# A conformer layer with product-key experts: both expert halves from fetched rows for the last 128 tokens, and a dense first half for 416

## The chip, the cores and the metric

The kernel runs on one core of one Trainium2 chip. The metric is the device time of one execution in microseconds (us). A core has TensorE (PE in the profile, PEld its weight loads), VectorE (DVE), ScalarE (ACT), GpSimd (POOL) and SyncE (SP), and 16 DMA engines that all queues share.

## The reference

One layer of an encoder for 544 tokens (a prompt of 512 and 32 of a running stream), model width 2048, all in fp32. The part around the change is the second half of the layer, a layer of single-neuron experts:

```python
def peer(h, w_pq, sub_k1, sub_k2, u_tab, v_tab):        # h = rms_norm(x, norm2_g)
        q = (xb @ w_pq).reshape(PEER_BLOCK, PEER_HEADS, PEER_DKEY).astype(f32)   # 8 heads, 128 wide
        s1 = jnp.einsum('thd,nd->thn', q[..., :half], sub_k1.astype(f32))        # 128 keys each
        s2 = jnp.einsum('thd,nd->thn', q[..., half:], sub_k2.astype(f32))
...
        sc, j = lax.top_k(cand, PEER_TOPK)                                       # 16 of 256 candidates
        idx = jnp.take_along_axis(cidx, j, axis=-1)                              # expert = i1 * 128 + i2
        g = jax.nn.softmax(sc, axis=-1)
        ue = u_tab[idx]
        ve = v_tab[idx]
        a = jnp.einsum('td,thkd->thk', xb, ue).astype(f32)
        wgt = (g * jax.nn.gelu(a, approximate=False)).astype(xb.dtype)
        return jnp.einsum('thk,thkd->td', wgt, ve)
```

There are 16384 experts, so u_tab and v_tab (peer_u, peer_v) are 16384 x 2048; a token uses 8 x 16 = 128 of them. Ahead of it stand a projection of 9216 columns with convolution and attention, two output projections that are merged with gates, `w_out`, and the residual.

## The kernel before

**Numbers.** Every large product is made of three fp32r products. ACT rounds a loaded block of weights (`w_raw`, 128x2048) to `w_hi` (L546), POOL makes the rest `w_lo = w_raw - w_hi` (L482), and PE adds hi·hi, lo·hi and hi·lo. A *unit* is one such block: 16 slices of 128 rows against 544 tokens, held as two halves of 272, so 96 matmuls (L1280). Weights and their parts have two buffers. Loops are hardware loops, two units a round, and engines meet only by semaphores that count; each engine runs its program in its written order.

**Stages.** Stage 1 (39 to 1093 us) has 72 units, in four head pairs of 18: projection, convolution on DVE (L877), attention. `evac` on DVE (L784 to L808) takes a unit's result out of PSUM, and the next unit but one needs that space. Then come merge (16 units, 1093 to 1317 us), out (16, to 1509), PQ (the query projection, 8, to 1603), U (128 units of peer_u, to 3216) and V (16 groups of 8 blocks of peer_v, to 4450).

**U stage.** Each unit gives 128 experts' activations for all 544 tokens: ACT copies them out of PSUM (L708), POOL scales them by the RMS factor `rs2` (L500), ACT applies Gelu (L712) and stores them to `a_scr`. The first 40 units have the top-k of five tiles of tokens on DVE between them (L1066 to L1120), eight units to a tile; PE waits for a tile's choice in a hook in the next tile's seventh unit (L1507 to L1509). After them follow 26 blocks of 16 tokens, three units each, in which one-hot matmuls (L1532) turn the chosen gates into a dense gate matrix `g_scr`; DVE makes the one-hot operands (L1147 to L1149) and takes the results (L1162, L1164). Ten units more end the stage.

**V stage.** For the first 416 tokens activations times gates are multiplied densely with peer_v, 384 matmuls of 416 columns a group (L1557). For the last 128 tokens POOL fetches for each of the 128 slots one row of peer_v per token (`rows`, L506, from `v_rows`) and the single activation (`elements`, L513, from `a_scr`), and DVE weighs them (L1202) and adds row times weight (`gather_add`, L1208). In this stage DVE makes `w_lo` (L1196).

**Rows of peer_v.** The table in `w_all` is stored in blocks for PE; `v_rows` is a copy of it as rows, made in stage 1 by SP: two DRAM-to-DRAM transfers of 1 MB for each unit (`rows_of`, L334), behind the unit's load of `w_raw` (L316), on SP's one queue.

Of the kernel before, what the change touches and what calls it, by code (L numbers as in the profile page):

```python
# [20 lines left out]
F32 = mybir.dt.float32  # L21
F32R = mybir.dt.float32r
# [4 lines left out]
P = 128  # L27
# [36 lines left out]
NVG = 3  # L64
# [36 lines left out]
def build(nc, w_all, x_t, consts, late, params, lams, keys_t, past_k, past_v, hist,  # L101
          y_t, k_t, v_n, cst_p, cst_s):
    ctx = ExitStack()
    with ctx:
# [44 lines left out]
        oraw = ay.take("oraw", [P, T])  # L149
        az = Area(MT, MEND - MT)  # L150
# [7 lines left out]
        rs1 = az.take("rs1", [P, T])  # L158

# [23 lines left out]
        h2_lo = ao.take("h2_lo", [P, KD, T], F32R)  # L183
        aq = Area(MT, MEND - MT)
# [8 lines left out]
        ab = au.take("ab", [P, 2, T])  # L193
        gb = au.take("gb", [P, 2, T])
        v_idx = au.take("v_idx", [P, SLOTS], U32)
        a_idx = au.take("a_idx", [P, SLOTS], U32)
        gate_g = au.take("gate_g", [P, SLOTS])
        a_el = au.take("a_el", [P, SLOTS])
        w_g = au.take("w_g", [P, SLOTS])
        gsum_g = au.take("gsum_g", [P, NH])  # L200
        p_col = au.take("p_col", [P, 1])
# [3 lines left out]
        g_hi = ag.take("g_hi", [P, T], F32R)  # L205
# [20 lines left out]
        oh2 = aw.take("oh2", [P, 8, NKEY], F32R)  # L226
        oh1 = aw.take("oh1", [P, 8, 2, NKEY], F32R)

        avx, avy = Area(X0, BIG), Area(Y0, BIG)
        acc = avx.take("acc", [P, KD, T])  # L230
        a_st = avy.take("a_st", [P, GRP, NT])
# [21 lines left out]
        g_scr = nc.dram_tensor("g_scr", (NGB, P, NKEY, GB), F32, kind="Internal").ap()  # L253
        v_rows = nc.dram_tensor("v_rows", (NGRP, GRP, P, DM), F32, kind="Internal").ap()
# [37 lines left out]
        ab_full, ab_scaled, gelu_done = sem("ab_full"), sem("ab_scaled"), sem("gelu_done")  # L292
# [12 lines left out]
        vg_loaded, vg_taken = [sem(f"vg_loaded{i}") for i in range(NVG)], sem("vg_taken")  # L305
        el_loaded = [sem("el_loaded0"), sem("el_loaded1")]
# [6 lines left out]
        def _(sp):  # L313
# [17 lines left out]
            def rows_of(hp, g, n):  # L331
# [43 lines left out]
            with sp.Fori(0, NH // 2) as hp:  # L375
                z_loads(hp)
# [1285 lines left out]
```

## Time and profile before

| what | value |
|---|---|
| median of 3 runs | 4459.39 us (4457.0 to 4462.22) |
| profiled execution, its time and its span | 4454.38 us, 4452.6 us |
| busy share of the span | PE 98%, DVE 67%, POOL 39%, ACT 24% |
| moved by DMA | 822.58 MB |
| mean granted clock of TensorE | 0.989 of full speed |

The span is from the first to the last instruction of the profiled execution. Busy times of PE are modelled and overlap (two matmuls in the pipe), so the pace of PE is read from the starts of its instructions. A `xN` behind an instruction says that N of them are drawn together. What ended an engine's idle time stands behind an arrow.

### The profile page before, as it was taken

The numbers are of one execution on the slowest core, as the hardware profiler recorded it, in microseconds if no ns is written. First come the engines' busy times: TensorE is split into PE (matmuls) and PEld (weight loads), VectorE is DVE, ScalarE is ACT, GpSimd is POOL, SyncE is SP. The second block draws the span as 40 slices with busy tenths as digits, with TensorE's granted clock in tenths as the row PEclk, the third lists the DMA queues.
The fourth block names the chain that finished last, engine by engine and source line by source line (L and its number), as shares of the span: only waits on it lengthen the run. The fifth ranks groups of instructions, "written<-read, shape, count | busy, mean of one in ns | idle before, by whom it ended". The sixth has DMA issues, their size and how long they took to land.

```text
span 4452.6 us, 78681 instructions
## 1 busy us (share of the span) xinstructions
PE 4351.6 (98%) x30758; PEld 4276.9 (96%) x30758; DVE 3003.3 (67%) x4653; ACT 1079.1 (24%) x1100; POOL 1758.2 (39%) x639
## 2 busy tenths in 40 slices
PE   8999999999999999999999999999989999999999
PEld 7999999999999999999999999999989999999999
DVE  5767656676762256557888888886268777877774
ACT  3332323322211122222222222222212121221221
POOL 3323323332333344444444444444544433444420
PEclk9999999999999999999999999999999999999999
DMA  6656566564333322222333333333577767776763
GB/s 241 235 191 229 197 234 229 188 227 164 106 136 135 110 95 108 108 106 102 133 126 136 131 130 135 134 135 128 198 277 264 291 261 292 266 296 258 282 253 126
DMA packets 332184, 822.58 MB, mean 185 GB/s; under 512 B 23152, under 2 KB 230768, under 8 KB 264688
## 3 DMA queue, kind: packets, MB, share of 16 engines
q1 hardware_dynamic: 279968, 608.53, 39.0%
q0 software_dynamic: 22528, 134.30, 7.4%
q10 hardware_dynamic: 29520, 77.40, 4.5%
q8 instruction: 119, 1.95, 0.2%
q14 instruction: 49, 0.40, 0.0%
HBM read 734.72 MB, written 219.66 MB: 214 GB/s over the span
## 4 chain that ended last, share of the span: by engine, by line
issue 56%; PE 21%; POOL 18%; DMA 3%; DVE 1%; POOLq 0%; ACT 0%; DVEq 0%; SPq 0%; ACTq 0%
PE pair L1557 21%; POOL w_lo L482 13%; POOL ab L500 4%; DMA a_el<-a_scr,a_idx 3%; POOL vg L506 1%; DVE ST L1208 1%; DVE acc L1192 0%; POOL a_el L513 0%; DMA xs<-x_t 0%; POOL xsq L488 0%; POOLq L481 0%; ACT h_hi L552 0%; POOLq L497 0%; POOLq L492 0%; DVE w_lo L1196 0%
## 5 line engine op out<-in xcount | busy, mean ns | idle before, releaser
L482 POOL TENSOR_TENSOR w_lo<-w_raw,w_hi 128x2048 fp32r<-128x2048 f32 x242 | 1118.0, 4620 | 1114.6 <-ACT w_hi L546 1114.6
L1280 PE MATMUL pair<-h_hi,w_hi 128*128 128x272 f32 x6656 | 1397.5, 291 | 12.8 <-issue 12.8
L1280 PE MATMUL pair<-h_hi,w_lo 128*128 128x272 f32 x6656 | 1381.5, 289 | 0.0
L1280 PE MATMUL pair<-h_lo,w_hi 128*128 128x272 f32 x6656 | 1377.0, 288 | 0.0
L1280 PEld LDWEIGHTS pair<-h_hi,w_hi 128*128 128x128 f32 x6656 | 1048.2, 189 | 21.1 <-issue 13.9
L1280 PEld LDWEIGHTS pair<-h_lo,w_hi 128*128 128x128 f32 x6656 | 1048.5, 189 | 0.0
L546 ACT ACTIVATE w_hi<-w_raw 128x2048 fp32r<-128x2048 f32 x368 | 703.8, 1913 | 1417.3 <-PE pair L1557 858.4
L1280 PEld LDWEIGHTS pair<-h_hi,w_lo 128*128 128x128 f32 x6656 | 1044.7, 189 | 0.0
L1557 PE MATMUL pair<-wt_hi,w_hi 128*128 128x416 f32 x2048 | 727.3, 355 | 49.4 <-DVE acc L1192 48.3
L1557 PE MATMUL pair<-wt_hi,w_lo 128*128 128x416 f32 x2048 | 728.7, 356 | 0.0
L1557 PE MATMUL pair<-wt_lo,w_hi 128*128 128x416 f32 x2048 | 722.6, 353 | 0.0
L506 POOL DMA_INDIRECT vg<-v_rows,v_idx x128 | 321.1, 2508 | 595.7 <-DVE ST L1208 584.9
L500 POOL TENSOR_TENSOR ab<-ab,rs 128x544 f32<-128x544 f32 x128 | 178.7, 1396 | 791.0 <-ACT ab L708 791.0
L1557 PEld LDWEIGHTS pair<-wt_hi,w_hi 128*128 128x128 f32 x2048 | 389.7, 190 | 57.3 <-DVE acc L1192 53.2
L1557 PEld LDWEIGHTS pair<-wt_lo,w_hi 128*128 128x128 f32 x2048 | 390.3, 191 | 6.3
L1557 PEld LDWEIGHTS pair<-wt_hi,w_lo 128*128 128x128 f32 x2048 | 389.5, 190 | 3.2
L708 ACT ACTIVATE ab<-pair 128x544 f32<-128x544 f32 x128 | 80.1, 626 | 1203.5 <-PE pair L1280 1203.5
L1148 DVE TENSOR_SCALAR oh<-late_sb,i_t,g_hi 128x128 fp32r<-128x128 f32 x416 | 356.5, 857 | 0.0
L877 DVE SCALAR_TENSOR_TENSOR xg<-u,params_sb,xg 128x512 f32<-128x512 f32 x464 | 338.6, 771 | 23.3 <-DVE xg L875 1.3
L1192 DVE TENSOR_TENSOR acc<-pair,acc 128x416 f32<-128x416 f32 x256 | 149.4, 588 | 277.0 <-PE pair L1557 218.0
L1208 DVE SCALAR_TENSOR_TENSOR ST<-vg,w_g,ST 128x2048 f32<-128x2048 f32 x128 | 300.6, 2348 | 2.9 <-DVE w_g L1202 2.9
L1196 DVE TENSOR_TENSOR w_lo<-w_raw,w_hi 128x2048 fp32r<-128x2048 f32 x126 | 287.9, 2285 | 13.3 <-ACT w_hi L546 13.3
(223 smaller groups left out, 3999.6 us busy)
## 6 DMA issues: line engine op xcount, KB each, us to landing
w_raw<-w_all SPq DMA_DIRECT2D x368, 1024.0 KB
v_rows<-w_all SPq DMA_DIRECT2D x128, 1024.0 KB, 8.8
a_scr<-gb ACTq DMA_DIRECT2D x128, 272.0 KB, 2.1
g_scr<-g_st ACTq DMA_DIRECT2D x26, 1024.0 KB, 4.1
a_st<-a_scr SPq DMA_DIRECT2D x16, 1664.0 KB, 8.4
gl_st<-g_scr SPq DMA_DIRECT2D x16, 1664.0 KB
gate_scr<-zb ACTq DMA_DIRECT2D x32, 272.0 KB, 2.2
gt<-gate_scr SPq DMA_DIRECT2D x32, 272.0 KB, 3.4
```

The costliest lines, as they stand in the source:

```text
L482: pool.tensor_tensor(w_lo[:, slot, :], raw[:, slot, :], w_hi[:, slot, :].bitcast(F32), ALU.subtract)\
L500: pool.tensor_tensor(ab[:, n, :], ab[:, n, :], rs2[:, :], ALU.mult).then_inc(ab_scaled, 1)
L506: pool.indirect_dma_start(vg[j % NVG][:, :], None, v_rows.rearrange("g c p d -> (g c p) d"), bass.IndirectOffsetOnAxis(v_idx[:, j:j + 1], ...
L546: act.activation(w_hi[:, slot, :], raw[:, slot, :], ACT.Copy).then_inc(hi_ready, 1)
L708: act.activation(two(ab[:, n, :]), PV[n], ACT.Copy).then_inc(ab_full, 1)
L877: own.by(V.scalar_tensor_tensor(xg[:, a:b], src, cw, xg[:, a:b], ALU.mult, ALU.add))
L1148: V.tensor_scalar(oh1[:, sl, 0, :], iota, c1, g_hi[:, bass.ds(t, 1)].bitcast(F32), ALU.is_equal, ALU.mult)
L1192: V.tensor_tensor(acc[:, d, 0:NT], PD[k], acc[:, d, 0:NT], ALU.add).then_inc(acc_added, 1)
L1196: V.tensor_tensor(w_lo[:, slot, :], raw[:, slot, :], w_hi[:, slot, :].bitcast(F32), ALU.subtract)\
L1208: V.scalar_tensor_tensor(acc_g, vg[x % NVG][:, :], w_g[:, bass.ds(s0 + x, 1)], acc_g, ALU.mult, ALU.add)\
L1280: last = mm(out[:, f, :], a, b[:, k, f * HT:(f + 1) * HT], start=(x == 0 and y == 0), stop=(x == n - 1 and y == 2))
L1557: last = mm(PD[k], a, r_[b][:, c, :], start=(c == 0 and y == 0), stop=(c == GRP - 1 and y == 2))
```

## The change

Five things are changed together.

1. **U for 416 tokens.** Units of peer_u are multiplied with the first 416 tokens only, 48 matmuls of 416 columns (`u_unit`). `h2` is scaled by `rs2` before PQ (DVE `h2_s`, ACT rounds, DVE subtracts, slice by slice), so ACT applies Gelu directly from PSUM (`u_slot`) and L500 and L708 fall away.
2. **Rows of peer_u.** In stage 1 SP also loads the 128 blocks of peer_u (`u_load`, 1 MB each, two a unit in 16 of a head pair's 18 units), DVE transposes each in 32x32 pieces (`turn`, at the head of `evac`), and SP stores it to `u_rows` by four transfers of 32 partitions (`u_store`). The copies to `v_rows` move to the loops of merge, out, PQ and U. The merge's inputs `c_all` and `o_lo` make room: they are stored to `c_scr` and `o_scr` in stage 1 and loaded again at its end.
3. **Dots.** For the last 128 tokens POOL fetches rows of peer_u (`fetch`, nine in a round of two gate blocks, three buffers `rows`) and DVE makes one dot product per slot with `h2_g` in PSUM (`dot`, 128x2048). 128 matmuls ahead of the gate blocks (`h2_turned`, at the end of unit 41) put `h2` there with tokens on partitions.
4. **Gate blocks.** They begin at unit 42 instead of 40. One-hot matmuls are fp32 with 128 columns, where they were fp32r with 256; L1148 falls away; the results are copied out by ACT (`gate_copy`) and no longer by DVE. DVE makes `w_lo` of every second unit there (L1248), POOL of the others.
5. **V stage.** Fetched activations and their weighing are gone: one Gelu over the dots on ACT and one product with the gates on DVE stand ahead of the stage.

```diff
--- before.py
+++ after.py
...
         SV, TOV = S[:, :, 0:HT], TO[:, :, 0:HT]
 
         def two(ap):
@@ -251,6 +260,9 @@
         x2_scr = nc.dram_tensor("x2_scr", (KD, P, T), F32, kind="Internal").ap()
         a_scr = nc.dram_tensor("a_scr", (NKEY, P, T), F32, kind="Internal").ap()
         g_scr = nc.dram_tensor("g_scr", (NGB, P, NKEY, GB), F32, kind="Internal").ap()
+        c_scr = nc.dram_tensor("c_scr", (KC, P, T), F32, kind="Internal").ap()
+        o_scr = nc.dram_tensor("o_scr", (KC, P, T), F32, kind="Internal").ap()
+        u_rows = nc.dram_tensor("u_rows", (NKEY, 4, 32, 4, DM // 4), F32, kind="Internal").ap()
...
+            def u_load(hp, i):
+                sp.dma_start(u_in[:, i % 2, :], w_all[bass.ds(hp * 32 + (i + U_PU), 1)].rearrange("a p n -> p (a n)"))\
+                    .then_inc(u_loaded[i % 2], 16)
+
+            def u_store(hp, i):
+                for q in range(4):
+                    sp.dma_start(u_rows[bass.ds(hp * 32 + i, 1), :, :, q, :].rearrange("a b i n -> i (a b) n"),
+                                 u_out[32 * q:32 * q + 32, i % 2, :].rearrange("p (b n) -> p b n", b=4)).then_inc(u_stored[i % 2], 16)
...
+                        for k in range(2):
+                            if n <= 16:
+                                sp.wait_ge(u_turned, hp * 32 + (2 * n + k + 1))
+                            if n < 16:
+                                u_load(hp, 2 * n + k)
+                            if 1 <= n <= 16:
+                                u_store(hp, 2 * n + k - 2)
...
+            for s in u_stored:
+                sp.wait_ge(s, 64 * NKEY // 2 + 1)
+            sp.wait_ge(o_stored, 16 * (NH - 1) + 1)
+            sp.wait_ge(c_stored, 32 * (NH - 1) + 1)
+            sp.dma_start(o_lo[:, 0:NH - 1, :].bitcast(F32), o_scr[0:NH - 1].rearrange("c p n -> p c n")).then_inc(o_loaded[0], 16)
+            sp.wait_ge(c_stored, 32 * NH + 1)
+            sp.dma_start(c_all[:, :, :], c_scr.rearrange("c p n -> p c n")).then_inc(c_loaded, 16)
+            sp.wait_ge(o_stored, 16 * NH + 1)
...
+            def turn(hp, i):
+
+                dve.wait_ge(u_loaded[i % 2], hp * 256 + 16 * (i // 2 + 1))
+                dve.wait_ge(u_stored[i % 2], hp * 1024 + (64 * (i // 2) + 1))
+                V.transpose(u_out[:, i % 2, :].rearrange("p (b k j) -> p k b j", b=4, k=KD), u_in[:, i % 2, :])\
+                    .then_inc(u_turned, 1)
...
             def evac(hp, r, i):
+
+                for k in range(2):
+                    if ZPH * r + i < 16:
+                        turn(hp, 2 * (ZPH * r + i) + k)
 
...
+            for k in range(KD + 1):
+                if k < KD:
+                    V.tensor_tensor(h2_s[:, k, :], h2_s[:, k, :], rs2[:, :], ALU.mult).then_inc(h2_scaled, 1)
+                if k > 0:
+                    dve.wait_ge(h2_rounded, k)
+                    V.tensor_tensor(h2_lo[:, k - 1, :], h2_s[:, k - 1, :], h2_hi[:, k - 1, :].bitcast(F32), ALU.subtract)\
+                        .then_inc(h2_ready, 1)
             with dve.Fori(0, NQ // 2) as v:
...
-            def elements(j):
-                b = j // PER_GRP
-                if b >= 2 and j % PER_GRP == 0:
-                    pool.wait_ge(el_loaded[b % 2], 16 * PER_GRP * (b // 2))
-                pool.indirect_dma_start(a_el[:, j:j + 1], None, a_scr.rearrange("c p (n o) -> (c p n) o", o=1),
...
+            def fetch(j):
+
+                if j >= NG:
+                    pool.wait_ge(row_taken, j - NG + 1)
+                table = u_rows.rearrange("c b i q n -> (c b i) (q n)") if j < SLOTS else v_rows.rearrange("g c p d -> (g c p) d")
+                pool.indirect_dma_start(rows[j % NG][:, :], None, table,
+                                        bass.IndirectOffsetOnAxis(v_idx[:, j % SLOTS:j % SLOTS + 1], 0))\
+                    .then_inc(row_loaded[j % NG], 16)
 
             pool.wait_ge(idx_ready, 1)
+            for s in u_stored:
+                pool.wait_ge(s, 64 * NKEY // 2 + 1)
+            pool.wait_ge(scores_taken, TT)
+            pool.wait_ge(chosen, TT)
+            j = 0
+            for v in range(NGB // 2):
+                for k in range(3):
+                    w = U_PU + U_G0 + 6 * v + 2 * k + 2
+                    for i in range(DOTS // 3):
+                        fetch(j)
...
-            def u_slot(v, n):
+            def u_slot(v, n, src):
                 m = v * 2 + n
                 act.wait_ge(unit_done, m + (1 + NZ + NO + NQ))
-                act.activation(two(ab[:, n, :]), PV[n], ACT.Copy).then_inc(ab_full, 1)
+                act.wait_ge(a_stored[n], v * 16 + 1)
+                act.activation(gb[:, n, :], src[n], ACT.Gelu).then_inc(ab_full, 1)
                 hi(v + (U_PU // 2 + 1), n)
-                act.wait_ge(ab_scaled, m + 1)
-                act.wait_ge(a_stored[n], v * 16 + 1)
-                act.activation(gb[:, n, :], ab[:, n, :], ACT.Gelu).then_inc(gelu_done, 1)
-                act.wait_ge(gelu_done, m + 1)
-                act.dma_start(a_scr[bass.ds(m, 1)].rearrange("a p n -> p (a n)"), gb[:, n, :]).then_inc(a_stored[n], 16)
+                act.wait_ge(ab_full, m + 3)
...
+            def gate_copy(v, gq):
+
+                b, t0 = gq // 4, 4 * (gq % 4)
+                act.wait_ge(grp_done, v * 8 + (gq + 1))
+                if gq % 4 == 0:
+                    act.wait_ge(g_stored[b], v * 16 + 1)
+                act.activation(g_st[:, b, :, t0:t0 + 4], ST[:, 2 + gq % 2, :].rearrange("p (c t) -> p c t", t=4), ACT.Copy)\
...
+            def dot(v, i):
+
+                j = v * DOTS + i
+                dve.wait_ge(row_loaded[i % NG], v * (16 * DOTS // NG) + 16 * (i // NG + 1))
+                buf = rows[i % NG]
+                V.scalar_tensor_tensor(buf[:, :], buf[:, :], 1.0, h2_g, ALU.mult, ALU.mult,
+                                       accum_out=dot_g[:, bass.ds(j, 1)]).then_inc(row_taken, 1)
+
             def g_round(v, more):
...
-                    b = gq // 4
-                    dve.wait_ge(grp_done, v * 8 + (gq + 1))
-                    if gq % 4 == 0:
-                        dve.wait_ge(g_stored[b], v * 16 + 1)
-                    part = (S, TO)[gq % 2][:, :, :].rearrange("p a n -> p (a n)").rearrange("p (t h c) -> p t h c", t=4, h=2)
-                    t0 = 4 * (gq % 4)
-                    dst = g_st[:, b, :, t0:t0 + 4].rearrange("p c t -> p t c")
-                    own.by(V.tensor_copy(dst, part[:, :, 0, :]))
-                    settle()
-                    V.tensor_tensor(dst, dst, part[:, :, 1, :], ALU.add).then_inc(grp_taken, 1)
-                    if more or gq < 6:
-                        one_hot(v, gq + 2)
-
-            one_hot(0, 0)
-            one_hot(0, 1)
+                def next_hot(gq):
+                    if more or gq < 4:
+                        dve.wait_ge(grp_done, v * 8 + (gq + 1))
+                        one_hot(v, gq + 4)
+
...
+            def u_unit(v, n, dst, hooks=None):
                 pe.wait_ge(lo_ready, v * 2 + (n + 1 + U_PU))
                 pe.wait_ge(ab_full, v * 2 + (n + 1))
-                product(PV[n], n, 0, range(KD), h2_hi, h2_lo, hooks).then_inc(unit_done, 1)
+                for k in range(KD):
+                    wh, wl = (w[:, n, k * P:(k + 1) * P] for w in (w_hi, w_lo))
+                    for y, (a, b) in enumerate(((wh, h2_hi), (wh, h2_lo), (wl, h2_hi))):
+                        last = mm(dst[n], a, b[:, k, 0:NT], start=(k == 0 and y == 0), stop=(k == KD - 1 and y == 2))
+                    if hooks and k in hooks:
+                        hooks[k]()
+                last.then_inc(unit_done, 1)
+
+            def h2_turned():
+
+                for k in range(KD):
+                    for q in range(4):
+                        for y, src in enumerate((h2_hi, h2_lo)):
+                            last = mm(PA[:, q, 32 * k:32 * k + 32], src[:, k, NT:T].bitcast(F32), ident[:, 32 * q:32 * q + 32],
+                                      start=(y == 0), stop=(y == 1))
+                last.then_inc(h2g_ready, 1)
```

On SP's queue, in stage 1, these rows stand between one load of weights and the next. Before:

```order
L316 DMA w_raw<-w_all 128x2048
L334 ISA
L334 DMA v_rows<-w_all 128x8x256
L334 ISA
L334 DMA v_rows<-w_all 128x8x256
L343 REGISTER_ALU
```

After, of which the second half repeats for the unit's second block:

```order
L331 DMA w_raw<-w_all 128x2048
L372 REGISTER_ALU
L355 ISA
L355 DMA u_in<-w_all 128x2048
L360 ISA
L360 DMA u_rows<-u_out 32x4x512
L360 ISA
L360 DMA u_rows<-u_out 32x4x512
L360 ISA
L360 DMA u_rows<-u_out 32x4x512
L360 ISA
L360 DMA u_rows<-u_out 32x4x512
```

Two copies have become two loads and eight stores, and a wait for DVE's transposes (`u_turned`) has come onto this queue behind each load of weights.

On DVE, in stage 1, this is the place between the last instruction of attention's softmax and `evac`'s first multiplication. Before:

```order
L851 SCALAR_TENSOR_TENSOR e<-e,small 128x256
L788 REGISTER_ALU
L796 REGISTER_ALU
L808 TENSOR_TENSOR zb<-pair,rs_74 128x544
```

After:

```order
L949 SCALAR_TENSOR_TENSOR e<-e,small 128x256
L873 REGISTER_ALU
L874 REGISTER_ALU
L875 STREAM_TRANSPOSE u_out<-u_in 128x16x4x32 x2
L886 REGISTER_ALU
L894 REGISTER_ALU
L906 TENSOR_TENSOR zb<-PA,rs_78 128x544
```

Two transposes, each behind waits for its load and for the four stores before it, have come ahead of the multiplication that frees the unit's PSUM.

On DVE, in the gate blocks, this is one stretch of a round of two blocks after the change (`rows` are the fetched rows, `oh` the one-hot operands, `PA` holds `h2_g`):

```order
L1248 TENSOR_TENSOR w_lo<-w_raw,w_hi 128x2048
L1254 ISA
L1256 ISA
L1256 SCALAR_TENSOR_TENSOR rows_133,dot_g<-rows_133,PA 128x2048
L1263 ISA
L1241 ISA
L1241 TENSOR_SCALAR oh_130<-late_sb,i_t 128x128
L1242 ISA
L1242 TENSOR_SCALAR oh_131<-late_sb,i_t,e_t 128x128
```

Before there were only L1147 to L1149 and the copies here; a split and nine dots a round have come in between, each dot behind a wait for its fetched row, and the one-hot operands stand behind them.

## Rows read from the trace of the kernel before

**Rows 1.** Windows by stage: us, busy us (instructions) per engine, clock, DMA share, GB/s.
```profile
39.00:1093.00 1054.00, 1041.16 (x7790) 993.79 (x7789) 690.48 (x986) 317.41 (x474) 326.27 (x72) 0.99 0.61 211
...
1603.00:3216.00 1613.00, 1612.05 (x12882) 1609.79 (x12881) 1162.28 (x2526) 403.64 (x411) 768.43 (x255) 1.00 0.35 126
3216.00:4450.00 1234.00, 1183.95 (x6160) 1166.46 (x6160) 892.33 (x887) 244.62 (x129) 456.30 (x258) 0.98 0.70 261
```

**Rows 2.** Timeline of PE, U stage: start us, us, instruction, count.
```profile
2107.74 0.28 PE L1532 MATMUL ST<-oh,oh 128*128 128x256 f32 x1
2107.86 0.41 PE L1280 MATMUL pair<-h_hi,w_hi 128*128 128x272 f32 x2
2108.11 0.41 PE L1280 MATMUL pair<-h_lo,w_hi 128*128 128x272 f32 x2
```

**Rows 3.** Waits, V stage: who, for whom, us in total, times, longest.
```profile
DVE w_g L1202 <- DMA a_el<-a_scr,a_idx: 89.7, 14, 14.3
...
PE pair L1557 <- DVE acc L1192: 48.3, 14, 11.4
```

**Rows 4.** Chain that ended last, its last piece: start us, us.
```profile
4376.84 72.55 PE pair L1557 x384
```

**Rows 5.** Timeline of PE, fp32 score matmuls in the U stage.
```profile
1704.26 3.50 PE L1499 MATMUL ST<-ksb,qp 64*128 64x128 f32 x32
1707.69 0.52 PE L1280 MATMUL pair<-h_hi,w_hi 128*128 128x272 f32 x2
```

**Rows 6.** Timeline of DVE, top-k of token tile 0, first and last instruction.
```profile
1707.89 1.22 DVE L1066 COPY sc<-ST 128x1024 f32<-128x1024 f32 x1 [20.32 <-PE ST L1499]
...
1767.73 2.29 DVE L1120 TENSOR_REDUCE isel<-wk 128x128 f32<-128x2048 f32 x1
```

**Rows 7.** Timeline of PE, the matmuls that wait for that top-k.
```profile
1782.96 0.27 PE L1509 MATMUL ST<-consts_sb,ssub 128*128 128x128 f32 x1
```

**Rows 8.** Groups by line on DVE, 2020 to 3080 us (busy us, mean ns; idle before).
```profile
L1149 DVE TENSOR_SCALAR oh<-late_sb,i_t,e_t 128x128 fp32r<-128x128 f32 x412 | 183.0, 444 | 0.0
L1147 DVE TENSOR_SCALAR oh<-late_sb,i_t 128x128 fp32r<-128x128 f32 x413 | 154.9, 375 | 0.0
```

**Rows 9.** Groups by line, V stage.
```profile
L1208 DVE SCALAR_TENSOR_TENSOR ST<-vg,w_g,ST 128x2048 f32<-128x2048 f32 x128 | 300.6, 2348 | 2.9 <-DVE w_g L1202 2.9
L1196 DVE TENSOR_TENSOR w_lo<-w_raw,w_hi 128x2048 fp32r<-128x2048 f32 x126 | 287.9, 2285 | 13.3 <-ACT w_hi L546 13.3
```

**Rows 10.** Timeline of DVE, stage 1 (in brackets idle before, and releaser).
```profile
779.93 1.97 DVE L877 SCALAR_TENSOR_TENSOR xg<-u,params_sb,xg 128x512 f32<-128x512 f32 x4
...
782.45 6.23 DVE L877 SCALAR_TENSOR_TENSOR xg<-u,params_sb,xg 128x512 f32<-128x512 f32 x4
```

**Rows 11.** Timeline of POOL in the same stretch.
```profile
783.02 4.55 POOL L482 TENSOR_TENSOR w_lo<-w_raw,w_hi 128x2048 fp32r<-128x2048 f32 x1 [10.09 <-ACT w_hi L546]
```

**Rows 12.** Windows inside stage 1 and the V stage.
```profile
400.00:600.00 200.00, 195.72 (x1486) 188.72 (x1485) 133.83 (x187) 62.19 (x87) 63.69 (x14) 0.99 0.61 208
...
3400.00:3800.00 400.00, 383.46 (x1985) 377.37 (x1984) 304.32 (x299) 80.53 (x42) 166.12 (x94) 0.98 0.74 276
```

**Rows 13.** DMA issues: KB each, median us from issue to landing.
```profile
v_rows<-w_all SPq DMA_DIRECT2D x128, 1024.0 KB, 8.8
...
g_scr<-g_st ACTq DMA_DIRECT2D x26, 1024.0 KB, 4.1
...
x_scr<-x ACTq DMA_DIRECT2D x16, 272.0 KB, 2.1
```

**Rows 14.** Timeline of PE, end of a head pair in stage 1.
```profile
829.56 0.79 PE L1280 MATMUL pair<-h_hi,w_hi 128*128 128x272 f32 x2 [4.53 <-issue]
...
834.61 0.41 PE L1280 MATMUL pair<-h_hi,w_lo 128*128 128x272 f32 x2
```

**Rows 15.** Timeline of PE, from stage 1 into the merge.
```profile
1100.51 0.64 PE L1280 MATMUL pair<-o_hi,w_hi 128*128 128x272 f32 x2 [2.30 <-DVE zb L808]
```

**Rows 16.** Timeline of DVE, from out into PQ.
```profile
1507.56 4.50 DVE L1022 COPY osq<-osum 128x544 f32<-128x544 f32 x1 [0.21 <-DVE osum L1019]
```

More of the change, by code:

```diff
@@ L158, in build @@
         rs1 = az.take("rs1", [P, T])
+        c_ts = az.take("c_ts", [P, TS])
         xs = Area(Y0, HALF).take("xs", [P, KD, T])
@@ L183, in build @@
         h2_lo = ao.take("h2_lo", [P, KD, T], F32R)
+        h2_s = Area(X0 + HALF, HALF).take("h2_s", [P, KD, T])
         aq = Area(MT, MEND - MT)
@@ L535, in _ @@
+            w = U_PU + U_G0 + BU * NGB + 1
+            while w < U_PV + 2:
+                pool.wait_ge(lo_ready, w)
+                lo(w, w % 2)
+                w += 1
+                for i in range(2):
+                    if j < SLOTS:
+                        fetch(j)
+                        j += 1
+            pool.wait_ge(rows_stored, 16 * NV)
+            for j in range(SLOTS, 2 * SLOTS):
+                fetch(j)
         @block.scalar
@@ new lines, in g_round @@
+            def g_round(v, more):
+                def next_hot(gq):
+                    if more or gq < 4:
+                        dve.wait_ge(grp_done, v * 8 + (gq + 1))
+                        one_hot(v, gq + 4)
+                un = v * 6 + (U_PU + U_G0 + 1)
+                dots = iter(range(DOTS))
+                for b in range(2):
+                    for i in range(BU):
+                        if (BU * b + i) % 2 == 0:
+                            split(un + (BU * b + i), 1)
+                        dot(v, next(dots))
+                        next_hot(4 * b + i)
+                        if i < 2 - b:
+                            dot(v, next(dots))
+                    next_hot(4 * b + 3)
@@ L1170, in _ @@
+            for gq in range(4):
+                one_hot(0, gq)
+            dve.wait_ge(h2g_ready, 1)
             with dve.Fori(0, NGB // 2 - 1) as v:
-                own.loop(v, 8)
                 g_round(v, True)
-            own.endloop(NGB // 2 - 1)
             g_round(NGB // 2 - 1, False)
+            for i in range(SLOTS - NGB // 2 * DOTS):
+                dot(NGB // 2, i)
             def prep(parity, c):
@@ L1214, in _ @@
                 prep(0, c)
+            dve.wait_ge(a_g_ready, 1)
+            own.by(V.tensor_tensor(w_g[:, :], gate_g[:, :], a_el[:, :], ALU.mult))
+            settle()
             dve.wait_ge(unit_done, NZ + NO + NQ + NU)
@@ L1218, in group @@
             def group(g, parity, more, slots, splits, pre=None):
-                s0, full, rounds, n_slots = slots
+                s0, rounds, n_slots = slots
                 for n in range(GRP):
@@ L1426, in merge_unit @@
                     product(PV[k], n, KC * k, range(KC), rhs_hi, rhs_lo, hooks and hooks[k]).then_inc(tile_done, 1)
-            with pe.Fori(0, NA // 4) as v:
+            for n in range(2):
+                merge_unit(0, n, 0, o_hi, o_lo, ({KC - 2: lambda: pe.wait_ge(o_loaded[1], 16)}, {KC - 1: mean}) if n == 0 else None)
+            with pe.Fori(1, NA // 4) as v:
                 for n in range(2):
```

281 lines of the change are left out of this document (150 added, 131 removed).

## The prediction, made before the changed kernel had run

> **What bounds the kernel now.** I read the windows by stage first. PE is busy in 1041 of the 1054 us of stage 1, in 1612 of 1613 us of U and in 1184 of 1234 us of V [rows 1]. So in U nothing but PE's own work counts; in V some 50 us are waits, and in stage 1 about 13. DVE stands at 690 of 1054 us in stage 1 and the DMA engines at a share of 0.61 with 211 GB/s [rows 1]: neither bounds now, and the change loads both. The timeline of PE gives the pace of U: a pair of 272-column matmuls starts every 0.25 us (2107.86, 2108.11 [rows 2]), so 48 pairs, a unit, take 12.0 us; the window's 1613 us less 49 for one-hot matmuls and 17 for scores (priced below) give 12.09 for each of 128 units. I take 12.02. The chain's last piece shows 416 columns: 384 matmuls in 72.55 us, 188.9 ns each [rows 4]. The waits of the V stage name DVE's `w_g` for fetched activations, 89.7 us in 14 groups, and behind it PE for DVE's `acc`, 48.3 us in the same 14 [rows 3].
>
> **U.** A unit becomes 48 x 188.9 ns = 9.07 us; 128 units give 128 x (12.02 - 9.07) = **-378 us**. Removed on ACT and POOL is work beside PE, worth nothing by itself; Gelu from PSUM takes the copy's place. Added:
> - One-hot matmuls become fp32. 32 passes of 128 columns in fp32 took 1707.69 - 1704.26 = 3.43 us [rows 5], a block's 16 matmuls have 32 such passes; the fp32r ones took 0.118 us each (2107.74 to 2107.86 [rows 2]), 1.89 a block. 26 x 1.54 = **+40**.
> - `h2_turned`: 256 passes of 32 columns. Nothing in the trace is this small; by columns it is a quarter of 107 ns, 7 us in all, and by passes 27. A pass of 32 columns still loads its weights, so I take **+22**.
> - The top-k. DVE takes 1707.89 to 1770.02, 62.2 us with its end [rows 6]; PE asks for it at 1782.96 [rows 7], 6.25 units after the scores, and finds it ready. 6.25 units are now 56.7 us, so PE waits 5.5 us, four times. A wait this long brings the half clock: behind the 4.53 us gap at 829.56 PE ran at the lower granted clock for some 5 us (a matmul pair at 0.45 us) before it returned to 0.25 [rows 14], a loss near 2. 4 x 7.2 = **+28**.
> - Gate blocks. A round of two blocks takes PE 6 x 9.07 + 2 x 3.43 = 61.3 us. DVE's round: 9 dots at 2.35 and 3 splits at 2.29 [rows 9] and 32 tokens' operands at 0.375 + 0.444 [rows 8], 54 us. That fits, but a dot waits for its fetched row, and with it the split behind it, for which PE waits. I take **+15** for 13 rounds, and **+5** for the 11 dots left at the end; 0 and +80 are the ends (a 6 us stall a round).
>
> Together -268.
>
> **V.** Without the activations' fetch its waits go, and groups run at the last one's pace: 16 x 72.55 + 2 = 1163 for 1234: **-71**. DVE's 892 us of the stage [rows 1] are 56 a group, inside 72, so the faster pace is not beyond it.
>
> **Seams.** Into PQ the rms copy (4.50 us on DVE [rows 16]) and the reciprocal now stand ahead of PE, with two slices of `h2_s` behind: **+15** (12 to 18). Into the merge PE waited 2.30 us at 1100.51 [rows 15]; now `c_all` and `o_lo` come back from DRAM: a 1 MB copy lands after 8.8 us, a store of 272 KB after 2.1 [rows 13]. **+13** (5 to 20).
>
> **Stage 1 decides.** A slot (one unit's time) is 1054 / 72 = 14.64 us; 64 of 72 slots get two blocks of peer_u.
> - *DMA.* Before, a slot moved 211 GB/s x 14.64 us = 3.1 MB: one load, two copies. Now it is three loads (3.15 MB), two blocks stored (2.1 MB) and some 0.3 MB of others. 208 GB/s at a share of 0.61 is 341 GB/s at full share in stage 1, and 276 at 0.74 is 373 in V [rows 12]. Loads and others: 3.45 MB / 373 = 9.3 us. The stores have no like in the trace: 32 partitions each. Best, they run as the rest: 5.6 us, slot 15.0. Worst, by landing times: 272 KB lands after 2.1 us, 1 MB after 4.1 [rows 13], so four quarters one by one take 8.4, 2.05 times as long: 11.5 us, slot 20.8. I take 1.67, nearer the worst since each SP transfer here is a quarter as large as any in stage 1: 9.4 us, slot **18.7**. The queue is SP's own, so loads of weights stand behind the stores, and the turn for the next block waits for the stores and stands ahead of `evac`: whatever the DMA lacks, PE waits for.
> - *DVE.* A transpose reads and writes 128x2048 once; the nearest rows are the split's 2285 ns and the dot's 2348 [rows 9]: two a slot, 4.6 us. DVE's 690 us become 985, 13.7 a slot. In a slot of 18.7 us it is hidden; in one of 14.64 only partly, since DVE already loses time when POOL splits: four taps took 1.97 us at 779.93 and 6.23 at 782.45 [rows 10], while POOL's split ran from 783.02 for 4.55 us [rows 11].
> - *Sum.* 64 x (18.7 - 14.64) = **+260**, PE at the lower clock for parts of it included, since the DMA sets the pace.
>
> The Trainium skill (*SBUF — State Buffer*, Door 1: The DMA port swizzle) speaks against the change: partitions 0 to 31, like 0 to 63, reach 8 of SBUF's 16 ports, 189 GB/s measured for 1 MiB against 328 with all 128, and two transfers on different partitions do not add up. By that ratio, 1.74, an estimate of the slot is 9.3 + 9.8 = 19.1 us, and stage 1 grows by 283. No row of this trace shows such a transfer.
>
> **The sum.** Span 4452.6 - 268 - 71 + 15 + 13 + 260 = 4402; the profiled execution's own time lies 1.8 above its span, and the median 5 above that: **4408**.
>
> **Rivals.**
> - *A: the stores run like the rest* (0.27). For: there are 16 engines, and a share of 0.61 has room. Against: the demand is 15.0 us for a slot of 14.64 even so, and DVE's turns are half exposed. Stage 1 +80 (0 to 119): 4228.
> - *B: the forecast* (0.45). Slots of 16.5 to 19.4; own range 4267 to 4453.
> - *C: stores at half rate, slower than before* (0.2). One mechanism: each store of a quarter takes 2.05 times its share of the engines, slot 20.8, stage 1 +394: 4542. It decides from a slot of 19.5 us, where +311 eats the -311 of all the rest. The skill's rule, above, gives 19.1, just short of it.
> - *D: the gate blocks get bound by DVE and the fetched rows* (0.08). With the copies gone DVE still has 54 of 61 us a round, and a row is asked for only when a buffer is free. At 6 us a round, +80 in place of +15 on B: 4473; on A still faster.
>
> **How the numbers follow.** About 0.2% (9 us) is what a measurement of this kernel tells from no change. Faster: A 0.27, B nearly all (0.43), a third of D: 0.73. Slower: C 0.18 and half of D: 0.22; the same: 0.05. The range leaves out A's best end and C's worst: 4200 to 4530. It is wide because two mechanisms of 300 us each stand against one another, and the trace prices just one of them.
>
> **What would show it.** Right: U units at 9.07 us, 128 of them; V near 1163; stage 1 from 39 to about 1353 us with the DMA share near 0.9 or above in its first 16 slots of a head pair, DVE's turns idle ahead for `u_in` or `u_rows`, and slots 17 and 18 of each head pair back at 14.6. A: stage 1 below 1180 us, share under 0.9. C: above 1400 us. Wrong in U: waits on PE for `w_lo` from DVE L1248 of more than 3 us a round, or top-k hooks without a gap. The prediction fails most easily by the stores' price: each tenth of the factor is 0.57 us a slot, 36 us in all.

## The result, and the profile after

| what | before | after |
|---|---|---|
| median | 4458.19 us (4 runs) | 4353.9 us (4348.5 to 4361.58, 4 runs) |
| ratio, 95% interval | | 0.9768 (0.9748 to 0.9788) |
| profiled execution: span, mean clock | 4452.6 us, 0.989 | 4356.1 us, 0.968 |
| moved by DMA | 822.58 MB | 1225.88 MB |

The change made the kernel 104 us faster; some 50 were forecast, and the time lies inside the range. The windows of the changed kernel, cut at the starts of its stages (stage 1, merge and out, PQ, U, V; columns as in [rows 1]):

```profile
39.00:1255.00 1216.00, 1079.01 (x7781) 1019.57 (x7779) 935.24 (x1119) 315.49 (x473) 330.50 (x72) 0.95 0.86 302
1255.00:1687.00 432.00, 405.31 (x3112) 401.90 (x3112) 200.05 (x210) 82.68 (x58) 148.08 (x32) 0.97 0.85 289
1687.00:1795.00 108.00, 100.80 (x769) 100.40 (x769) 24.42 (x38) 23.44 (x22) 31.96 (x7) 0.95 0.69 245
1795.00:3174.00 1379.00, 1339.86 (x7407) 1321.61 (x7407) 995.85 (x2190) 377.08 (x388) 549.84 (x221) 0.97 0.72 272
3174.00:4354.00 1180.00, 1167.70 (x6160) 1155.91 (x6160) 889.60 (x872) 241.77 (x126) 303.90 (x125) 0.99 0.73 275
```

U has become 1379 us and is still PE's, V 1180. Stage 1 has become 1216, and there PE is busy for 1079 of them: 137 us of waits where there were 13. For as many matmuls PE's busy time has itself grown from 1041 us to 1079, with the granted clock at 0.95 where it was 0.99: some 38 of the 162 us more are the lower clock behind the waits. The DMA engines are at 0.86 and DVE at 935 of 1216, so neither total is full. What stands at PE's waits in this stage (who, for whom, us in total, times, longest; the first row is DVE's own wait ahead of the transposes):

```profile
DVE u_out L875 <- DMA u_rows<-u_out: 92.8, 30, 7.7
...
PE ST L1394 <- ACT sq L649: 50.5, 10, 12.9
...
PE ST L1465 <- DVE e L949: 47.1, 20, 5.4
```

PE waits mainly in two kinds of places: for `sq` once per head pair, the largest single waits, and for softmax's `e` (below). Units are counted from 0 and slots from 1 here, so that `evac` of unit 9 runs while PE works on the eleventh slot. This is the place of the first kind. The timeline of DVE there (idle before and its releaser in brackets), and of PE:

```profile
489.67 4.50 DVE L875 STREAM_TRANSPOSE u_out<-u_in 128x2048 f32<-128x2048 f32 x2
494.09 0.69 DVE L906 TENSOR_TENSOR zb<-PA,rs 128x544 f32<-128x544 f32 x1
502.51 2.31 DVE L875 STREAM_TRANSPOSE u_out<-u_in 128x2048 f32<-128x2048 f32 x1 [7.73 <-DMA u_rows<-u_out]
510.02 2.31 DVE L875 STREAM_TRANSPOSE u_out<-u_in 128x2048 f32<-128x2048 f32 x1 [5.20 <-DMA u_rows<-u_out]
512.25 0.69 DVE L906 TENSOR_TENSOR zb<-PA,rs 128x544 f32<-128x544 f32 x1
```

```profile
513.89 2.17 PE L1394 MATMUL ST<-sq,consts_sb 128*128 128x272 f32 x4 [11.19 <-ACT sq L649]
```

DVE comes to the second unit's turns straight behind the first unit's `zb` here, because the first is late behind attention's normalization (L885 and L887 in the kernel before). Before the change the two, L808, were 3.4 us apart at this place:

```profile
430.68 3.55 DVE L885 RECIPROCAL rstd<-rstd 128x544 f32<-128x544 f32 x1
434.26 4.54 DVE L887 TENSOR_TENSOR oraw<-oraw,rstd 128x544 f32<-128x544 f32 x1
...
440.26 0.72 DVE L808 TENSOR_TENSOR zb<-pair,rs 128x544 f32<-128x544 f32 x1
443.68 0.72 DVE L808 TENSOR_TENSOR zb<-pair,rs 128x544 f32<-128x544 f32 x1 [2.70 <-PE pair L1280]
```

The second unit's transposes need the buffers of the first's, and so the landing of stores that SP had only just issued. SP's rows in the changed kernel:

```profile
492.72 2.22 SPq L360 DMA_DIRECT2D u_rows<-u_out  x4
...
495.75 4.55 SPq L360 DMA_DIRECT2D u_rows<-u_out  x4
```

From issue to landing these stores take 7.0 us in the median, 2.8 to 10.6. The time of one slot, read as the distance of every 96th matmul of the projection, in the second head pair (18 slots, us; before, after):

```
before 13.6 13.9 13.9 14.3 14.6 15.4 16.1 14.4 13.9 12.0 13.9 13.9 14.3 14.6 15.4 16.1 14.4 18.4
after  13.4 13.9 14.4 14.8 15.9 20.7 18.6 15.7 14.0 14.1 29.7 14.2 14.8 17.1 21.1 17.6 15.7 18.6
```

So stage 1 did not get slots of 18.7 us, as forecast. Half of them are within 1 us of before; the eleventh has 15 to 16 us more, the sixth and fifteenth 5 to 6, where PE waits for softmax (`e`) on DVE. The mean of all 72 is 16.9.

### The profile page after: what moved, and what is told of

Read it like the earlier page. It is cut to its first block, busy times and chain, and to the rows that moved or that the text cites. A ratio compares the mean times of both kernels' runs of the same rounds, so it can differ in the third digit from the quotient of the medians.

```text
span 4356.1 us, 69382 instructions
## 1 busy us (share of the span) xinstructions
PE 4112.9 (94%) x25286; PEld 4014.4 (92%) x25286; DVE 3072.1 (71%) x4447; ACT 1059.1 (24%) x1090; POOL 1385.7 (32%) x472
## 2 busy tenths in 40 slices
DMA packets 444255, 1225.88 MB, mean 281 GB/s; under 512 B 32800, under 2 KB 256800, under 8 KB 343968
## 4 chain that ended last, share of the span: by engine, by line
PE 53%; issue 33%; POOL 6%; DVE 6%; DMA 1%; ACT 0%; SPq 0%; POOLq 0%; ACTq 0%; DVEq 0%
PE ST L1686 27%; PE ST L1602 17%; POOL w_lo L542 6%; PE PA L1602 3%; PE ST L1661 2%; PE PA L1380 2%; PE PA L1612 1%; DVE wk L1210 1%; DMA w_raw<-w_all 1%; DVE cand L1180 1%; DVE wk L1214 0%; DVE isel L1218 0%; DVE ti L1176 0%; DVE wk L1172 0%; DVE ti L1179 0%
## 5 line engine op out<-in xcount | busy, mean ns | idle before, releaser
L1686 PE MATMUL ST<-wt_hi,w_hi 128*128 128x416 f32 x2048 | 719.9, 352 | 24.2 <-DVE wt_lo L1295 12.9
L1686 PE MATMUL ST<-wt_hi,w_lo 128*128 128x416 f32 x2048 | 724.7, 354 | 0.0
L1686 PE MATMUL ST<-wt_lo,w_hi 128*128 128x416 f32 x2048 | 716.9, 350 | 0.0
L1380 PE MATMUL PA<-h_hi,w_hi 128*128 128x272 f32 x2496 | 548.7, 302 | 26.6 <-issue 12.9
L1602 PE MATMUL ST<-h_hi,w_hi 128*128 128x416 f32 x1408 | 532.8, 378 | 11.8 <-POOL w_lo L542 11.8
L1380 PE MATMUL PA<-h_hi,w_lo 128*128 128x272 f32 x2496 | 527.5, 294 | 0.0
L1380 PE MATMUL PA<-h_lo,w_hi 128*128 128x272 f32 x2496 | 527.0, 293 | 0.0
L1602 PE MATMUL ST<-h_lo,w_hi 128*128 128x416 f32 x1408 | 498.7, 354 | 0.0
L1602 PE MATMUL ST<-h_hi,w_lo 128*128 128x416 f32 x1408 | 495.8, 352 | 0.0
L1380 PEld LDWEIGHTS PA<-h_hi,w_hi 128*128 128x128 f32 x2496 | 407.4, 195 | 36.0 <-issue 28.1
L1248 DVE TENSOR_TENSOR w_lo<-w_raw,w_hi 128x2048 fp32r<-128x2048 f32 x165 | 377.3, 2286 | 79.0 <-PE PA L1612 58.6
L875 DVE STREAM_TRANSPOSE u_out<-u_in 128x2048 f32<-128x2048 f32 x128 | 291.4, 2297 | 106.5 <-DMA u_rows<-u_out 92.8
## 6 DMA issues: line engine op xcount, KB each, us to landing
gl_st<-g_scr SPq DMA_DIRECT2D x16, 1664.0 KB, 16.2
```

Source lines behind the costliest of these rows:

```text
L875: V.transpose(u_out[:, i % 2, :].rearrange("p (b k j) -> p k b j", b=4, k=KD), u_in[:, i % 2, :])\
L1248: V.tensor_tensor(w_lo[:, slot, :], raw[:, slot, :], w_hi[:, slot, :].bitcast(F32), ALU.subtract)\
L1380: last = mm(out[:, f, :], a, b[:, k, f * HT:(f + 1) * HT], start=(x == 0 and y == 0), stop=(x == n - 1 and y == 2))
L1602: last = mm(dst[n], a, b[:, k, 0:NT], start=(k == 0 and y == 0), stop=(k == KD - 1 and y == 2))
L1686: last = mm(PD[k], a, r_[b][:, c, :], start=(c == 0 and y == 0), stop=(c == GRP - 1 and y == 2))
```

## The experiments

Each edit is against the changed kernel; `...` in a diff stands for lines left out. "Merge at" is the start of the merge's first matmul of out-projection weights, the end of stage 1: 1100.5 before, 1255.3 in the changed kernel. Numbers 4, 11 and 12 ran four or five times, all others once. Where an edit leaves stage 1 alone, this mark returns within 1 us (1255.1 in number 7, 1256.0 in number 8).

**1. No rows at all.**

```diff
-                                u_load(hp, 2 * n + k)
-                                u_store(hp, 2 * n + k - 2)
...
-                        turn(hp, 2 * (ZPH * r + i) + k)
...
-                table = u_rows.rearrange("c b i q n -> (c b i) (q n)") if j < SLOTS else v_rows.rearrange("g c p d -> (g c p) d")
+                table = w_all.rearrange("u p n -> (u p) n") if j < SLOTS else v_rows.rearrange("g c p d -> (g c p) d")
```

> Stage 1 without the rows of peer_u: no load, no transpose, no store; the dots fetch rows of the same size and number from the first 16384 rows of the weight table instead, so their values are not the reference's. It gives the whole price of the rows in stage 1. Both theories expect the merge's first matmul back from 1255 to between 1095 and 1110 us and a span near 4205 (4195 to 4215), with U and V within 5 us of the changed kernel's. If the merge began later than 1130, something other than the rows (the stores of c_all and o_lo, or the weights' load) would carry part of stage 1's growth.

Merge at 1083.7, span 4237.6. The price of the rows is 172 us, and stage 1 without them is 17 us shorter than before the change, 11 less than the lower end expected: the last slot of the first three pairs takes 15.6 to 15.8 us where it took 18.1 to 18.6. The copies of peer_v have left this stage, which is the likely reason; no run moves them alone. The span was 33 us longer than expected: six groups of V had gaps of 5.8 to 6.1 us on PE behind late weights, which the changed kernel has not. Why the loads were late in this build I did not find out.

**2. Quick turns.**

```diff
-                V.transpose(u_out[:, i % 2, :].rearrange("p (b k j) -> p k b j", b=4, k=KD), u_in[:, i % 2, :])\
+                V.tensor_copy(u_out[:, i % 2, 0:32], u_in[:, i % 2, 0:32])\
...
```

> Stage 1 with DVE's transposes replaced by copies of 32 of 2048 columns (the stored rows are wrong, loads, stores and all waits stand as they are). DVE theory (a turn's 2.25 us stands ahead of what PE waits for, and a slot waits for its two stores to land where DVE's evacuations are bunched): the sixth and fifteenth slot of a head pair fall from 21 to 15.5 to 17 us, the eleventh keeps 22 us or more, the merge begins 50 to 95 us earlier than 1255. DMA theory (the prediction's: the stores' price paces the slots): the same bytes move, stage 1 stays within 15 us.

Merge at 1181.7: 74 us earlier. The sixth slot fell to 16.2 to 19.1 us, in part less than expected, and the eleventh stayed at 26.4 to 27.6. The same bytes were moved, so the stores' throughput does not pace the stage as the prediction had it; and 98 us over the run without rows are left that are not the transposes' duration.

**3. One store of 128 partitions.**

```diff
-                for q in range(4):
-                    sp.dma_start(u_rows[bass.ds(hp * 32 + i, 1), :, :, q, :].rearrange("a b i n -> i (a b) n"),
-                                 u_out[32 * q:32 * q + 32, i % 2, :].rearrange("p (b n) -> p b n", b=4)).then_inc(u_stored[i % 2], 16)
+                sp.dma_start(u_rows[bass.ds(hp * 32 + i, 1)].rearrange("a b i q n -> (a b) (i q) n").rearrange("b p n -> p b n"),
+                             u_out[:, i % 2, :].rearrange("p (b n) -> p b n", b=4)).then_inc(u_stored[i % 2], 64)
```

> Each block of peer_u stored by one transfer from 128 partitions instead of four from 32, the same bytes in the same runs of 2 KB, but to other places of the table (the rows are wrong). DMA theory with dear 32-partition stores: the merge begins 60 us or more earlier than 1255 and the DMA share of stage 1 falls from 0.86 to under 0.8. DVE and round-trip theory: at most 30 us earlier, and that from the eleventh slot, where the turn waits for stores to land.

Merge at 1237.4, 18 us earlier; the eleventh slot 27.1 to 28.5. Dear stores would have given 60 or more.

**4. The wrong slot left free.**

```diff
...
+                n = ZPH * r + i
+                m = n if n < 10 else n - 1
                 for k in range(2):
-                    if ZPH * r + i < 16:
-                        turn(hp, 2 * (ZPH * r + i) + k)
+                    if n != 10 and m < 16:
+                        turn(hp, 2 * m + k)
```

> The turns of a head pair skip the eleventh slot and use the seventeenth, which was free; loads and stores follow. Round-trip theory: the eleventh slot falls from 28.8 to about 14 to 16 us in all four head pairs, the seventeenth grows by 1 to 3, the span falls by 40 to 55 us to about 4305, ratio to the kernel before near 0.966. DMA theory: the demand is only moved, total within 10 us of the changed kernel.

4347.59 us, ratio 0.9746 (0.9726 to 0.9767), merge at 1242.7; the eleventh slot stayed at 28.7 to 29.8. The expectation failed, and its trace shows why: the late turns were still there. Timeline of DVE in this run:

```profile
488.65 4.50 DVE L876 STREAM_TRANSPOSE u_out<-u_in 128x2048 f32<-128x2048 f32 x2
493.07 0.69 DVE L909 TENSOR_TENSOR zb<-PA,rs 128x544 f32<-128x544 f32 x1
501.43 2.31 DVE L876 STREAM_TRANSPOSE u_out<-u_in 128x2048 f32<-128x2048 f32 x1 [7.67 <-DMA u_rows<-u_out]
```

They are those of unit 9, the second head's first, evacuated while PE works on the next; I had freed unit 10.

**5. Unit 9 left free** (the same edit with 9).

> The trace of the run before this one shows that the late turn belongs to evac of unit 9 of a head pair (the second head's first), 8 us behind the turns of unit 8, and not to unit 10's, which that run had freed. Here unit 9 has no turns; units 10 to 16 have them. Round-trip theory: the slot of 28.8 us falls to 14 to 17 us in all four pairs, the span to 4295 to 4315. If the wait for the stores only moves to unit 10's turns, the slot behind it grows and the span stays above 4335.

Span 4309.9, merge at 1207.5: 48 us earlier, and the eleventh slot takes 15.3 to 15.6 us. The slot behind it grew to 16.8 to 18.4. The 48 us hold the duration of unit 9's transposes as well as their wait, but number 2 had taken that duration away and left the slot at 26.4 us and more: most of it is the wait.

**6. Turns behind zb.** The three lines that call `turn` stand at the end of `evac` instead of at its head.

> Both turns of a slot stand behind the multiplication that frees the unit's PSUM (zb) instead of ahead of it. What PE waits for is then late by no turn of its own slot, but the work behind it (reciprocals, attention's softmax) still is. Round-trip theory: PE's gap of 11.2 us at the second head's start shrinks to about 4 us or less, since zb no longer waits for the stores; the sixth and fifteenth slot stay above 18 us; span 4290 to 4330. If the order inside evac does not matter, within 10 us of the changed kernel.

Span 4280.0, 10 us below the expected range; merge at 1177.9: 77 us earlier, with nothing taken out. Waits of stage 1 in this run:

```profile
DVE u_out L875 <- DMA u_rows<-u_out: 153.4, 59, 8.0
...
PE ST L1393 <- ACT sq L649: 26.3, 4, 6.7
...
PE ST L1464 <- DVE e L948: 23.3, 9, 4.0
```

DVE waits longer for the stores than in the changed kernel (153.4 us for 92.8), PE for both of its causes half as long. The same transfer and the same wait cost 77 us less when the instruction that frees PSUM is not queued behind them. The gap at the second head shrank to 6.2 to 6.7 us, where 4 or less were expected, and the sixth slot fell to 17.5 to 18.3 us, a little more than expected. But for the stage's last slot, the longest is now the twelfth, 22.4 to 23.3.

**7. h2_turned in fp32r.** The small matmuls read `h2_hi` and `h2_lo` as they are and an identity that ACT has rounded:

```diff
...
-                            last = mm(PA[:, q, 32 * k:32 * k + 32], src[:, k, NT:T].bitcast(F32), ident[:, 32 * q:32 * q + 32],
+                            last = mm(PA[:, q, 32 * k:32 * k + 32], src[:, k, NT:T], ident_r[:, 32 * q:32 * q + 32],
```

> The 128 small matmuls of h2_turned as fp32r (one pass each) with a rounded identity, the same result: 128 passes where there were 256. In the changed kernel they took 49.5 us, at 0.21 us a pass since TensorE's clock fell to 0.5 there. If a pass is bound by its weight load and the clock stays at 0.5: 128 x 0.21 = 27 us, span 22 us shorter (4334). If the clock holds: 14 us and 35 us shorter. The prediction's price was 0.086 us a pass.

Span 4333.6, 22.5 us shorter: 128 passes from 2220.4 to 2245.0, 0.19 us each on average, with weight loads that went from 188 to 333 ns as the clock fell. In the changed kernel the windows before and over the 256 passes are:

```profile
2205.00:2217.50 12.50, 12.50 (x68) 12.38 (x67) 4.14 (x11) 2.32 (x2) 7.58 (x4) 1.00 0.33 106
2217.60:2267.20 49.60, 49.60 (x258) 49.60 (x257) 0.00 (x0) 2.31 (x2) 1.70 (x2) 0.56 0.22 88
```

PE counts as busy in every one of the 49.6 us, and the granted clock is 0.56 of full speed on average: 1.00 up to 2223, then 0.50, the lower of its two levels (1.2 GHz), over all the rest. A pass starts every 0.11 us before 2223 and every 0.21 us behind it.

**8. The order of loads at the tail of U.**

```diff
...
-            load_ag(0)
-            pq_pu_loads(g_end, (NQ + NU) // 2)
+            load_a(0)
+            pq_pu_loads(g_end, g_end + 1)
+            load_g(0)
+            pq_pu_loads(g_end + 1, (NQ + NU) // 2)
...
-            load_ag(1)
             for n in range(GRP):
                 sp.wait_ge(lo_ready, n + 1 + U_PV)
                 load_w(U_PV // 2 + 1 + n // 2, n % 2)
+                if n == 2:
+                    load_ag(1)
```

> Only the order of SP's loads around the seam between U and V is changed: the second of the two large loads of gates and activations (1.7 MB each) comes after two more blocks of weights, and the next group's pair after the third block of group 0. DMA-order theory: the gap of 11.75 us before the last U units goes to 0 to 3 us, the 12.9 us before the first V group to 0 to 8, the 11.25 in it to 0 to 3; together 20 to 33 us, span 4323 to 4336. If the fetched rows and not the loads are late there, under 8 us.

Span 4332.1, 24 us shorter. Of the gaps in the changed kernel,

```profile
3140.94 0.71 PE L1602 MATMUL ST<-h_hi,w_hi 128*128 128x416 f32 x1 [11.75 <-POOL w_lo L542]
...
3173.87 0.71 PE L1686 MATMUL ST<-wt_hi,w_hi 128*128 128x416 f32 x1 [12.90 <-DVE wt_lo L1295]
```

the first is 1.25 us here and the third (11.25 us, in V's first group) is gone; the second grew to 16.1, where 0 to 8 were expected. By the trace it is DVE's preparation of the first group's weights behind the last fetched rows (49.2 us of waits for them in this run, 58.2 in the changed kernel), which the order of loads does not reach; no run takes these rows away.

**9 and 10. Each block stored twice**, to price a store where the DMA engines are full: by eight transfers of 32 partitions, or by two of 128.

```diff
-                for q in range(4):
+                for to in (u_rows2, u_rows):
+                    for q in range(4):
...
```

> Each block of peer_u is stored twice, by eight transfers of 32 partitions (the second set to a table that nothing reads; results unchanged), so that the DMA engines must set the pace and the stores' price can be read. A slot is 9.3 us of loads and others by the prediction's rates plus two times the stores' 5.6 us times a factor. Cheap stores (factor 1 to 1.2): slots of 20.5 to 23 us, the merge begins between 1460 and 1620 us. The prediction's factor of 1.67: slots of 28 us, the merge begins after 1900 us.

> The same doubling, with transfers from 128 partitions (rows wrong, as in the run with one such store). Against the doubled 32-partition stores it gives what the partition count costs. If 32 partitions are dear by 1.7 or more: stage 1 some 350 us or more shorter than with eight small ones. If the share of 16 engines is all that counts: within 60 us.

Merge at 1556.7 with the small ones, as cheap stores would have it, and 1420.8 with the large: 136 us apart, between the two expectations. Stage 1 of both, in this order:

```profile
39.00:1556.70 1517.70, 1153.75 (x7780) 1090.91 (x7779) 925.62 (x1119) 315.73 (x473) 328.63 (x72) 0.86 0.96 330
```

```profile
39.00:1420.80 1381.80, 1123.11 (x7784) 1059.03 (x7784) 919.95 (x1120) 315.79 (x473) 328.90 (x72) 0.90 0.95 363
```

Engine time is the time of all packets divided by 16, that is the share times the length. Number 9 took 1450 us of it in stage 1, the changed kernel 1049: 128 more blocks cost 401 us, 3.1 us a block, 1.12 times the 2.8 us that the prediction called the best case. With 128 partitions it is 1307 - 1000 = 307 us (numbers 10 and 3), 2.4 a block.

The ratio of the two, 1.31, is not the stores' own price, for the loads' packets changed along with them. In the trace a block's store is 512 packets of 2048 bytes and a load of 1 MB 128 packets of 8192. The store's packets take 2.96 us of engine time a block in the changed kernel and 2.92 in number 9; with 128 partitions they take 2.71 (number 3) and 2.73 (number 10). So in their own packets 32 partitions cost 1.07 to 1.09 times as much as 128. The rest is in the loads beside them, a packet of which takes 389 ns in number 9 and 336 in number 10. A load takes 2.98 us in the changed kernel: the stores run like the rest, and neither ratio is near 1.67. The Trainium skill's 189 and 328 GB/s for 32 and 128 partitions at 1 MiB (*SBUF — State Buffer*, Door 1: The DMA port swizzle), a ratio of 1.74, have the right sign here, but not the size, in a queue of four quarters behind one another with loads between them; the measurement decides. The edit changes the number of transfers, four for one, together with the partitions, and no run tells the two apart.

**11 and 12. What the parts give together.** Number 11 has turns behind zb, the fp32r passes and the order of loads, and spreads `h2_turned` over unit 41, 8 passes behind each of its 16 slices:

```diff
-            u_unit(TT * TOPK_UNITS // 2, 1, PD, {KD - 1: h2_turned})
+            u_unit(TT * TOPK_UNITS // 2, 1, PD, {k: (lambda k=k: h2_turned(k, k + 1)) for k in range(KD)})
```

Number 12 is without that spreading, but leaves unit 9 free of turns.

> Turns behind zb, h2_turned in fp32r and spread over the slices of unit 41, and the tail's order of loads. The parts alone gave 76, 22 and 24 us; they lie in different stretches, so they should add: 4354 - 122 = 4232, and the spreading another 5 to 13 if the clock holds: 4215 to 4240, ratio to before 0.945 to 0.951.

> As the run before, with unit 9 of each head pair free of turns as well and h2_turned in fp32r but not spread. With turns behind zb the gap at the second head is 6.2 us and the slot of 22.4 to 23.3 us is now the twelfth; freeing unit 9 should shorten it by 4 to 8 us in each pair: 15 to 30 us, 4205 to 4225. If the softmax of the second head is what is late, nothing.

Number 11: 4227.07 us, ratio 0.9481 (0.9457 to 0.9506), as expected. Its unit 41 with the 128 passes:

```profile
2138.60:2161.50 22.90, 22.90 (x176) 22.81 (x174) 0.09 (x1) 2.75 (x4) 7.53 (x4) 1.00 0.58 231
```

22.9 us less 9.07 for the unit are 13.8, 0.108 a pass, with the clock at 1.00 throughout, where number 7 had the same passes in one row and the clock fell. Number 12: 4191.24 us, ratio **0.9407 (0.9383 to 0.9431)**, faster than both kernels, and 14 us below the expected range. Merge at 1134.5, 48 us earlier than in number 11, more than the 15 to 30 expected: PE's waits for `sq` are gone from its stage 1, and the twelfth slot takes 13.9 us. Its windows of stage 1, and of V from the first matmul:

```profile
39.00:1134.00 1095.00, 1048.59 (x7780) 997.35 (x7779) 823.83 (x1119) 317.49 (x473) 329.98 (x72) 0.98 0.94 335
...
3019.00:4187.00 1168.00, 1165.14 (x6160) 1153.31 (x6160) 889.72 (x873) 241.79 (x126) 302.61 (x125) 1.00 0.74 277
```

The same bytes now go through in 1095 us at a share of 0.94: this stage is near what the DMA engines allow. Their engine time is 1024 to 1057 us in every kernel that stores the rows once by quarters (1034 here); at number 9's share of 0.96 that is some 1080 us, an estimate. Of the 172 us that the rows cost, number 12 gets 121 back with all rows in place.

## Why the prediction was right or wrong

**The failed step is "The stores have no like in the trace ... I take 1.67 ... slot 18.7".** It gave stage 1 +260; measured is +155 to the merge's first matmul. Two things in it were off. The price of a store was 3.0 us a block (2.96 by its packets, 3.1 by number 9) and not 4.7. And the mechanism behind it, that the DMA's throughput paces all 64 slots alike, was not what ran. With the measured price the prediction's own sum gives a slot of 9.3 + 5.9 = 15.2 us and +36 for stage 1, an estimate, so such a sum leaves some 120 of the 155 us unexplained. Of the 172 us that the rows cost, DVE's 2.3 us a turn carry 74 (number 2), unit 9's turns, mostly by their wait for stores issued a few us before, 48 (number 5), and 77 hang on the order inside `evac` alone (number 6); the parts overlap and do not add. That the time fell inside the range is luck: a price too high stood in for a wait that was not in the sum. The prediction had that sentence ("the turn for the next block waits for the stores and stands ahead of `evac`"), but took it as a way for throughput to reach PE. In the runs it acts as a latency, and it costs where DVE's evacuations follow one another closely; the rows of such a place, two L808 3.4 us apart (shown above), were in the trace of before and I did not look for them.

**Right by place, off in size:**

- *The rivals.* B's range for the slots (16.5 to 19.4) holds the mean of 16.9, and its own range of time the result, but for another reason. C, stores at half rate, is excluded by number 9. A was right in price, stores like the rest, and not in time (+155 for its 0 to 119): neither the wait for the landing of stores nor the order in `evac` stood in it.
- *A turn's duration* was right: 128 transposes, 2297 ns on average, forecast 4.6 us a pair. What I called hidden in a slot of 18.7 us was not.
- *U*: -234 for -268. The unit is at 9.07 us. The waits for top-k are 3.6 to 3.7 us, four times, where 5.5 stood in the sum. The one-hot matmuls cost +49 for +40: with them a unit of the gate blocks takes 10.33 us on average. `h2_turned` is 49.5 us for 22: a pass takes 0.11 us at the full clock (28 us in all, about the forecast's price by passes), and the clock fell. The gate blocks have no gap on PE (0 for +15), so rival D did not occur, though DVE waited 130 us for rows there. The tail had 11.75 + 12.90 us for +5. The first comes from large loads ahead of weights on SP's queue (number 8), which stood in no term; the second stands behind the last fetched rows, and number 8 did not shorten it.
- *V*: -53 for -71. Its groups have no gap from the second on, as forecast; the first keeps a gap of 11.25 us, which before had too (11.35 us at 3246.84) and which I had counted as gone with the fetched activations. Number 8 removed it by the order of loads.
- *Seams*: from the merge's first matmul to U +36, and the gap ahead of it is 9.26 us for 2.30 [rows 15]: 43 for 28. PE waited 5.05 us for `o_lo` and 6.73 for `h_lo`.
- *What the v_rows copies cost in stage 1* stood at nothing; without them and without the new rows the stage is 17 us shorter than before (number 1).

Together -96.5 us of span: 155 + 36 - 234 - 53.

**Open:** why six groups of V had gaps in number 1. What number 1's 17 us are. And the 51 us that number 12's stage 1 has over that without rows: the sixth and fifteenth slots still take 17.5 to 19 us, where PE waits for softmax, and a share of 0.94 allows little more.

## What to carry to other kernels

Price a new transfer in a loop by two numbers: its bytes against the share that the engines have left, and its round trip against the shortest distance of two uses of its buffer; read that distance at the place where the consumer is bunched, not from the mean. An instruction that waits for such a transfer belongs behind the one that frees another engine's buffer, even if its own wait grows by that. And where many tiny matmuls are needed, put them between large ones.

## What the runs showed of the hardware

- Matmuls of 32 columns one behind another: PE busy without a gap, granted clock down to 0.50, 0.11 us a pass before it fell and 0.21 behind it. The same matmuls, eight at a time between three of 416 columns (numbers 7 and 11): clock 1.00, 0.108 us a pass.
- Stores of 256 KB from 32 partitions, four in a row: 2.9 to 3.0 us of engine time for 1 MB in their own packets, 7.0 us in the median from issue to landing; one store of 1 MB from 128 partitions: 2.7 us. With full engines stage 1 moved 330 GB/s (small stores, share 0.96) and 363 (large, 0.95).
- DVE's transpose of 128x2048 fp32 in 32x32 pieces takes 2.30 us, as much as a subtraction of that size (2.29, L1248).
